# Unread products of a constant block on TensorE in the first microseconds of a three-block transformer kernel

## The reference, cut to what matters

```python
h = rmsnorm(x, g_mix_pre[l])
(a_q, a_k, a_v, b_cq, b_ckv, b_kr, c_q, c_k, c_v) = jnp.split(h @ w_in[l], IN_SPLITS, axis=-1)
...
qb = (rmsnorm(b_cq, mla_q_norm_g[l]) @ mla_w_q_up[l])
kvb = (rmsnorm(b_ckv, mla_kv_norm_g[l]) @ mla_w_kv_up[l])
...
xo = cross_attention(rmsnorm(x, g_x_pre[l]), rmsnorm(mem, g_x_mem[l]), w_xq[l], w_xkv[l], w_xo[l])
```

## Time and profile before

| what | value |
|---|---|
| median of 3 runs | 1760.07 us (1758.36 to 1760.36) |
| the profiled execution | 1760.31 us, its span 1758.5 us |
| TensorE busy in the span | 1587.2 us (90%) |
| VectorE, ScalarE busy | 802.2 us (46%), 372.9 us (21%) |
| mean DMA rate | 220 GB/s over the span |

### The profile page before, as it was taken

One profiled execution on the slowest core, in us unless ns is written; L12 is line 12 of the kernel. 1 busy time (PEld: TensorE's weight loads), 2 busy tenths in 40 slices (PEclk: granted clock), 3 DMA queues, 4 the chain that ended last, 5 costly groups with the idle time before them and its releaser, 6 DMA issues.

```text
span 1758.5 us, 25942 instructions
## 1 busy us (share of the span) xinstructions
PE 1587.2 (90%) x10710; PEld 1077.5 (61%) x10710; DVE 802.2 (46%) x1622; ACT 372.9 (21%) x941; POOL 2.2 (0%) x6
## 2 busy tenths in 40 slices
PE   8999999999999999999999999999999767667665
PEld 5877878884488786888648778888853112101111
DVE  5676567565577765766656575242421000000001
ACT  4262131110325422311002561111211000000001
POOL 0000000000000000000000000000000000000000
PEclk9999999999999999999999999999999867777777
DMA  9314325354542242544444232221878999999997
GB/s 393 126 73 145 143 106 222 144 191 167 202 169 96 95 170 72 195 181 157 180 173 162 102 102 116 74 75 51 346 323 351 422 420 421 420 422 420 421 421 320
DMA packets 55520, 386.35 MB, mean 220 GB/s; under 512 B 6256, under 2 KB 6768, under 8 KB 10480
## 3 DMA queue, kind: packets, MB, share of 16 engines
q1 hardware_dynamic: 53424, 375.16, 54.1%
q10 hardware_dynamic: 1984, 9.57, 1.4%
HBM read 383.65 MB, written 1.05 MB: 219 GB/s over the span
## 4 chain that ended last, share of the span: by engine, by line
PE 72%; DMA 22%; DVE 3%; ACT 2%; issue 1%; SPq 0%; DVEq 0%; ACTq 0%
PE ps L205 53%; DMA arena<-in_stream 15%; DMA ring<-in_stream 6%; PE ps L2313 3%; PE ps L1063 2%; PE ps L1552 2%; PE ps L209 1%; PE ps L1162 1%; PE ps L713 1%; PE ps L1195 1%; PE ps L1221 1%; PE ps L1653 0%; PE ps L614 0%; PE ps L1003 0%; PE ps L2395 0%
## 5 line engine op out<-in xcount | busy, mean ns | idle before, releaser
L205 PE MATMUL ps<-arena 128*128 128x256 f32 (+4 forms) x2364 | 539.8, 492 | 72.5 <-DMA arena<-in_stream 62.8
L205 PEld LDWEIGHTS ps<-arena 128*128 128x128 f32 (+1 forms) x2364 | 304.2, 170 | 267.2 <-DMA arena<-in_stream 141.7
L205 PE MATMUL ps<-ring,arena 128*128 128x256 f32 (+5 forms) x1172 | 323.9, 499 | 34.7 <-DMA ring<-in_stream 30.2
L205 PE MATMUL ps<-arena,ring 128*128 128x256 f32 (+1 forms) x1212 | 274.4, 374 | 0.0
L205 PEld LDWEIGHTS ps<-ring,arena 128*128 128x128 f32 (+1 forms) x1172 | 177.9, 174 | 155.2 <-issue 70.5
L205 PEld LDWEIGHTS ps<-arena,ring 128*128 128x128 f32 x1212 | 216.2, 191 | 35.5 <-issue 9.6
L2649 PE MATMUL ps<-arena 128*32 128x512 f32 x218 | 147.3, 780 | 0.0
L2871 DVE TENSOR_TENSOR arena<-arena,ps 128x512 f32<-128x512 f32 x8 | 5.5, 687 | 307.5 <-PE ps L2649 307.5
L1110 ACT ACTIVATE arena<-arena,small 128x256 f32<-128x256 f32 x112 | 55.7, 498 | 69.6 <-DVE small L1097 53.2
L1699 ACT ACTIVATE arena<-arena 128x512 f32<-128x512 f32 x20 | 12.6, 630 | 179.4 <-DVE arena L1755 179.4
L1063 PE MATMUL ps<-arena 64*128 64x256 f32 (+3 forms) x256 | 46.8, 392 | 0.8 <-DVE arena L1093 0.5
(11 more groups left out here) (458 smaller groups left out, 1975.6 us busy)
## 6 DMA issues: line engine op xcount, KB each, us to landing
arena<-in_stream SPq DMA_DIRECT2D x160, 1024.0 KB, 24.4
ring<-in_stream SPq DMA_DIRECT2D x155, 1024.0 KB, 6.4
spare<-in_stream SPq DMA_DIRECT2D x16, 1024.0 KB, 26.5
par<-in_stream SPq DMA_DIRECT2D x8, 1024.0 KB, 27.0
const<-in_stream SPq DMA_DIRECT2D x8, 1024.0 KB, 26.5
par<-in_layer_par ACTq DMA_DIRECT2D x3, 1664.0 KB, 7.3
par<-in_stream SPq DMA_DIRECT2D x8, 512.0 KB, 25.4
const<-in_stream SPq DMA_DIRECT2D x8, 512.0 KB, 24.7
```

The source lines that it names most:

```text
L205: ins = self.pe.e.matmul(out, lhsT, rhs, start=start, stop=stop)
```

## The change

Two groups of products are added on TensorE, five of 128x512 ahead of everything and seven of 128x256 between the transposes of x's block 0 and the first projection. Both operands are the same block of ones, which VectorE sets with a memset after its first one; the result goes to the last bank of `p.dve_tiles` and is never read. The block is the space of `p.cq`. TensorE waits for the memset, and the wait for the constants moves behind the first five. Nothing is removed.

```diff
@@ -96,6 +96,7 @@
 WARM = 36
+START_IDLE, HEAD_IDLE = 5, 7
@@ -884,6 +885,7 @@
     p.cq = p.take(NB, 384)
+    p.idle_rows = flat(p.cq)[:, 0:P + 512]
@@ -1817,9 +1819,17 @@
+def idle_products(p, pe, n, width):
+
+    for _ in range(n):
+        pe.e.matmul(p.dve_tiles.banks[-1][:, 0:width], p.idle_rows[:, 0:P], p.idle_rows[:, P:P + width])
+
+
 def layer_pe(p, pe, w, l):
     ready = token_rows(p, l)
     block_columns_pe(p, pe, w, 0, p.x, ready(0))
+    if l == 0:
+        idle_products(p, pe, HEAD_IDLE, 256)
     pe.e.wait_ge(p.sem("layer_params"), l * 16 + 16)
@@ -2080,6 +2090,7 @@
     dve.e.memset(p.small[:, 254:255], 1.0).then_inc(dve.event("one"), 1)
+    dve.e.memset(p.idle_rows, 1.0).then_inc(dve.event("one"), 1)
     dve.e.wait_ge(p.sem("layer_params"), 16)
@@ -3491,6 +3502,9 @@
             w = Weights(p, pe)
+            p.stage = "start"
+            pe.e.wait_ge(p.sem("one"), 2)
+            idle_products(p, pe, START_IDLE, 512)
             pe.e.wait_ge(p.sem("const_loaded"), 16)
```

## The result

Slower, by a little: median 1762.97 us (1760.3 to 1765.34, 9 runs) against 1759.66 us (1758.07 to 1761.82, 9 runs), a ratio of 1.0018 with a 95% interval of 1.001 to 1.0027. That is +3.3 us, inside the stated range (1758.3 to 1763.4 us) and inside the 0.2% that was called "same", but two and a half times the +1.28 us of the sum, and above the bounds of the forecast itself (+0.4 to +2.0 us). The profiled execution's span is 1762.0 us, 3.5 us more than before.

The account below looks back on a forecast made before the run. TensorE and VectorE were taken to arrive together at the latent transposes. VectorE's chain through mem, ready at 37.82 against 36.54 us, gave +1.28 us: 1761.6 us on the profile, 1761.35 on the median, stated as 1761.4; range 1758.3 to 1763.4 us.

Parts of the forecast that it names:

- the sum: At the latent transposes TensorE is ready at 34.87 us, VectorE at 37.82; the later decides: +1.28 us against 36.54.
- Which chain decides: At the latent transposes, VectorE's chain through the load of mem decides, made 1.36 us later, not TensorE's own path.
- The slack: Before the latent transposes: TensorE could have begun at 36.46 us and began at 36.54, so both engines arrive together, 0.08 us.
- steps 1 to 3: Kernel start: memset ends near 1.48 us, five products end at 8.17, x's transposes slip 1.85 us, mem's chain 1.36 us.
- One for one from issue to landing: Load of mem: issue moves from 10.40 to about 11.8 us, and its landing is counted as late by the same amount.
- Rival B: Load of mem is hidden behind the weights' queue, landing stays at 22.50 us; 0.08 us faster, 1760.0 us; chance 0.12.
- step 4: Seven products behind x's transposes take 3.0 us, end at 12.05; cost 1.4 us on TensorE, nothing on VectorE's chain.
- step 5: First projection at the upper clock: first eight records and transposes 3.67 instead of 6.74 us; TensorE's path 1.67 us early.
- Rival C: TensorE's path decides at the latent transposes, no 2.95 us wait arises; 1.67 us gained, 1758.4 us; chance 0.12.
- rival D: At the start, unread products of constants do not raise the clock; everything 7.2 us later, 1767.3 us; chance 0.04.
- From there on all is driven by TensorE's chain: Behind the latent transposes VectorE's take-over (43.72 us) and hand-back (48.32 us) simply move along with the shift.
- list of things that would show it wrong: Signs: mem landing at 22.5 us; no new wait and VectorE early; 416-wide records 0.69 us apart after 17 us; a later-stage change.

Follow-up runs that it names:

- second profile: The changed kernel run and profiled once more with nothing altered; 1762.98 us against 1759.75 us for the kernel before, ratio 1.002.

## Why the prediction was right, and where it was not

**Which chain decides.** Right. The slack was put at 0.08 us; 22.50 + 13.92 us gives 0.12 us. The chain of waits of the page had named TensorE alone, and the run with mem late moves the time by as much as the change without touching TensorE's instructions.

**The start products (steps 1 to 3).** TensorE started at 1.62 us (1.65 expected) and the memset took 0.59 us (at most 0.61). The first record took 1.02 us, the others 0.85 us. By the spacing of the records the rise came near 7.5 us in the first profile (bounds 4.5 to 7.55, middle 6.15) and near 5.4 us in the second: the middle was a guess, no more. x's transposes began at 8.90 and 7.89 us (7.3 to 8.9, 8.17 taken); in the profile without head products, whose start products are the same, at 9.05 us, so the upper bound was a little short.

**One for one from issue to landing.** Nearly. The issue moved by 2.10 us and the landing by 1.59 us; in the second profile by 1.09 and 0.62 us. In all thirteen profiles mem landed 11.6 to 12.2 us after its issue, whether it was issued at 6.5 or at 12.7 us, so the half microsecond lies within what this delay varies by. Rival B is refuted: the landing is not hidden. The Trainium skill, "DMA: Bandwidth & Descriptors", "Queues, rings and completion order", has each engine take turns between the queues that have work; that the landing follows the issue agrees with it.

**The head products (step 4).** 3.02 us, 3.0 expected, and off the path, as the run without them shows.

**The gain (step 5).** TensorE's last product ahead of the latent transposes ended at 38.00 - 2.21 = 35.8 us. Counted as the prediction did, from start to start, the last two records of 128x384 started at 34.97 us and took 0.65 us of TensorE's time, so it was ready at 35.6 us, not 34.87 us: the rise came 1.3 us later than taken, and with it the start products ended 0.7 us later. Its wait by the same count was 2.4 us, 2.95 us expected. Rival C is refuted by the wait; rival D, that constants do not raise the clock, by the records of 0.43 us from 7.6 us on.

**The sum.** L was to be +1.28 us and was +1.46 us. That this is so close is in part luck: the issue of mem was 2.10 us late where 1.36 us was taken, and 0.51 us of that did not reach the landing; in the second profile L was only +0.50 us. That the time lies in the stated range is owed to its margin for scatter and not to the sum. The step that failed is the sentence behind it: "From there on all is driven by TensorE's chain". It counted the new wait as idle time that costs nothing and did not ask what TensorE's clock does in it. The term that is missing is the fall of the clock behind the wait, 1.67 us where it occurs. The material for it was at hand in the trace of before. The lower level of the stage at 1316 us stood behind a wait; TensorE's timeline of before has it in brackets:

```profile
1313.97 0.60 PE L2612 MATMUL ps<-const,small 128*16 128x128 f32 x2 [2.18 <-DVE small L3429]
```
In the prediction's own list of things that would show it wrong, a low clock was only looked for in the first projection.

**What stays open.** The measured +3.3 us (about +1.8 to +4.8 us by the interval) is more than the mean of what the two profiles show at H, +3.1 and +0.5 us; that mean, 1.8 us, is the lower end of the interval. The stage near 1002 us took 1.5 and 1.6 us more in them than in the kernel before, which brings them to +4.6 and +2.2 us there. Whether that is chance or the change makes the bad case more frequent there, one or two profiles of each kernel cannot tell. How often the clock falls in the wait is open in the same way; 17 timed runs of the changed kernel reach from 1760.3 to 1766.96 us, over 6.7 us, and those of the kernel before beside all these kernels from 1757.27 to 1762.41 us, over 5.1 us; that fits a loss that is present in some only, and does not show it.

## What to carry to other kernels

Work that is put in front of an engine "while it waits anyway" delays what that engine releases first; here ScalarE's issue of a load hung on TensorE's transposes, VectorE hung on that load, and TensorE on VectorE. Before adding work that only keeps TensorE's clock up, find the second chain that arrives at the next meeting of engines, and move its transfers out of the way first. And a wait is not free for TensorE just because another engine decides: price the clock that may fall behind it.

## What the runs showed of the hardware

**The clock falls behind short waits, and not by their length alone.** Idle times of 2.21, 2.74 and 4.25 us ahead of the latent transposes were followed by the lower level, idle times of 1.22, 2.27 and 2.75 us were not. The fall came 0.1 to 0.2 us after TensorE had gone on, and cost about 1.65 us each time (H - L of 13.58 and 13.59 us against 11.91 to 11.95 us). An idle time of 2.2 us was enough once, and one of 2.75 us was not. Near 1002 us TensorE was idle for 1.5 us in all thirteen profiles, and in eleven of them the clock fell in that wait or within 2 us behind it, in two it did not.

**Constants count.** Products of a block of ones brought TensorE to the upper level by their end, or within one record of it, in all seven profiles that had the start products, and x's transposes behind them ran 0.11 us apart. The 36 transposes of the identity went from 0.50 to 1.00 with nothing else on TensorE. The Trainium skill, "TensorE: Matmul & The Clock Gate", Part 4, says that the full clock does not engage for transposes; these rows do not agree.

**The clock column has no value for the start.** It says 1.00 at the start, before and after, while the records are spaced by the lower level (0.85 us for 128x512, 0.69 us for 128x416); in the stretch behind the wait the same column says 0.55 and agrees with the spacing.
